# Second attention of a transformer encoder: scores two blocks ahead are issued before the transposes of the present block

## The reference

```python
for qb in range(S // Q_BLOCK):              # 8 blocks of 128 queries
    q0 = qb * Q_BLOCK
    n_keys = q0 + Q_BLOCK                   # causal by chunks of 64
    s = (jnp.einsum('bqhd,bkhd->bhqk', q_nope[:, q0:n_keys], k_nope[:, :n_keys])
         + jnp.einsum('bqhr,bkr->bhqk', q_rope[:, q0:n_keys], k_rope[:, :n_keys])).astype(F32) * scale
    p = _masked_softmax(s, _chunk_mask(q0, n_keys)[None, None])
    outs.append(jnp.einsum('bhqk,bkhe->bqhe', p.astype(v.dtype), v[:, :n_keys]))
```

## Time and profile before

| | |
|---|---|
| runs shown | 3392.67, 3393.78, 3395.44 us; median 3393.78 |
| profiled execution, its own time | 3393.93 us |
| span of its instructions | 3392.2 us (so 1.73 us lie around it) |
| TensorE busy | 2859.6 us, 84% |
| VectorE busy | 1621.3 us, 48% |
| ScalarE busy | 1252.5 us, 37% |
| GpSimd busy | 302.0 us, 9% |
| mean granted TensorE clock | 0.910 of full speed |

### The profile page before, as it was taken

How to read it: one execution, slowest core, us unless ns; L and a number is a source line. 1 busy time by engine, 2 the same in 40 slices (tenths; PEclk the granted TensorE clock), 3 DMA queues, 4 the chain that set the end, 5 groups by cost and what they waited for, 6 DMA issues and landing times. The chain is left out here.

```text
span 3392.2 us, 38273 instructions
## 1 busy us (share of the span) xinstructions
PE 2859.6 (84%) x12732; PEld 2275.8 (67%) x12732; DVE 1621.3 (48%) x2801; ACT 1252.5 (37%) x2185; POOL 302.0 (9%) x314
## 2 busy tenths in 40 slices
PE   1778888877786999999994888888785999999995
PEld 1556555654564888888873677777673788888883
DVE  3454554454335434343456377777726323232325
ACT  0355655555305212121205356656514313121213
POOL 2000000000000000000044222222100000000000
PEclk9789888887697999999996899999987999999996
DMA  5312211112311322223222111111330111111111
GB/s 199 126 41 63 63 44 60 59 56 96 123 40 37 93 74 87 85 74 95 70 67 74 22 27 27 31 29 26 114 116 13 50 50 43 49 49 49 47 40 50
DMA packets 268778, 216.65 MB, mean 64 GB/s; under 512 B 36967, under 2 KB 244118, under 8 KB 268702
## 3 DMA queue, kind: packets, MB, share of 16 engines
q1 hardware_dynamic: 251662, 156.98, 15.6%
q0 software_dynamic: 17040, 58.73, 5.6%
HBM read 186.28 MB, written 33.59 MB: 65 GB/s over the span
## 5 line engine op out<-in xcount | busy, mean ns | idle before, releaser
L1543 PE MATMUL PA<-U,W 128*128 128x512 f32 x3840 | 969.5, 409 | 143.1 <-DVE W L1031 46.2
L1543 PEld LDWEIGHTS PA<-U,W 128*128 128x128 f32 x3840 | 747.9, 197 | 317.8 <-issue 100.1
L1543 PE MATMUL SC<-U,W 128*128 128x512 f32 x2064 | 484.0, 394 | 27.4 <-DVE U L1345 23.9
L639 ACT ACTIVATE W<-raw 128x1024 fp32r<-128x1024 f32 (+1 forms) x207 | 201.2, 975 | 778.5 <-PE PA L1543 360.9
L1543 PEld LDWEIGHTS SC<-U,W 128*128 128x128 f32 x2064 | 392.8, 191 | 112.1 <-issue 26.1
L1543 PE MATMUL PA<-H,W 128*128 128x512 f32 x1536 | 355.1, 390 | 0.0
L1543 PE MATMUL SC<-H,W 128*128 128x512 f32 x1536 | 353.4, 389 | 0.0
L1543 PEld LDWEIGHTS SC<-H,W 128*128 128x128 f32 x1536 | 288.4, 188 | 59.8
L1543 PEld LDWEIGHTS PA<-H,W 128*128 128x128 f32 x1536 | 287.5, 188 | 59.6
L1031 DVE TENSOR_TENSOR W<-raw,W 128x1024 fp32r<-128x1024 f32 (+1 forms) x207 | 244.8, 1185 | 117.9 <-ACT W L639 117.3
L1113 DVE TENSOR_TENSOR H<-TB,H 128x512 fp32r<-128x512 f32 (+3 forms) x216 | 122.7, 568 | 162.3 <-ACT H L682 162.2
(11 more groups left out here) (213 smaller groups left out, 3200.5 us busy)
## 6 DMA issues: line engine op xcount, KB each, us to landing
raw<-in_ffn_w SPq DMA_DIRECT2D x128, 512.0 KB, 4.1
ada<-in_ada_w POOLq DMA_DIRECT2D x96, 512.0 KB, 4.7
U<-attention_out SPq DMA_DIRECT2D x4, 3584.0 KB, 16.8
raw<-in_da_w_qkv SPq DMA_DIRECT2D x24, 512.0 KB, 4.8
attention_out<-ostage SPq DMA_DIRECT2D x32, 256.0 KB, 2.5
X<-residual SPq DMA_DIRECT2D x2, 4096.0 KB, 16.4
attention_out<-ostage SPq DMA_DIRECT2D x64, 128.0 KB, 2.3
X<-in_x SPq DMA_DIRECT2D x2, 2048.0 KB, 9.0
```

Of the source, the lines that this page charges most:

```text
L639: nc.scalar.activation(W[:, slot, 0, 0:kt * P], raw[:, slot, 0:kt * P], ACT.Copy).then_inc(w_hi, 1)
L1543: ins = mm(bank, W[:, slot, a, kt * P:(kt + 1) * P], moving(b, kt)[:, cols], start=kt == first and (a, b) == SPLIT[0], stop=kt == last and ...
```

## The change

Two edits. In each step TensorE issues the scores of block s + 2 first and the transposes of block s second, where it was the other way round. And the probabilities get four SBUF buffers in place of two, since the exponential of block s + 2 is no longer ordered behind the transposes of block s; the two more are rows 2 and 3 of the tile X, which nothing else uses at that time. The queues of ScalarE, VectorE, GpSimd and SyncE keep their order. No instruction is added or removed.

```diff
-        prob1 = [X[:, 0, :], X[:, 1, :]]
+        prob1 = [X[:, k, :] for k in range(4)]
...
-                nc.scalar.activation(prob1[s % 2][:, 0:n], SC[s % 2][:, 0:n], ACT.Exp, bias=neg_max(s),
+                nc.scalar.activation(prob1[s % 4][:, 0:n], SC[s % 2][:, 0:n], ACT.Exp, bias=neg_max(s),
                                      accum_out=row_sum(s)).then_inc(a1["p_ready"], 1)
...
-                    ins = transpose_to(t1_bank(p, ix)[:, (b % 4) * P:(b % 4 + 1) * P], prob1[s % 2][:, b * P:(b + 1) * P])
+                    ins = transpose_to(t1_bank(p, ix)[:, (b % 4) * P:(b % 4 + 1) * P], prob1[s % 4][:, b * P:(b + 1) * P])
...
                 for s in range(NQ):
-                    turn1(h, p, s, 0)
-                    if s >= 4:
-                        turn1(h, p, s, 1)
                     if s + 2 < NQ:
                         scores1(h, p, s + 2)
                     elif proj:
                         scores1(h + 1, 1 - p, s + 2 - NQ)
+                    turn1(h, p, s, 0)
+                    if s >= 4:
+                        turn1(h, p, s, 1)
                     if s == 0:
```

## The result

The changed kernel takes 3431.01 us (median of 4 runs, 3426.14 to 3433.51) against 3394.61 us for the kernel before (4 runs): 36.4 us or 1.1% slower, ratio 1.0106 with a 95% interval of 1.0089 to 1.0124. The profiled execution took 3433.51 us, its span is 3431.8 us and its mean granted clock 0.901. The second attention holds nearly all of the difference.

What follows compares the result with a forecast made beforehand. The prediction took the chain zigzagging between ScalarE and VectorE as the bound, not TensorE. Its terms 12.2 + 1.1 + 9.9 = 23.2 us, added to 3393.9, gave 3417, 0.7% slower; the range ran from 3404 to just over 3430.

Steps and rivals of the forecast that it cites:

- step 5: Sixth step of a head: scores fill TensorE's two bank waits, TensorE arrives 0.99 us sooner, nothing waits for it; gain 0.
- step 7: Last step of a head: TensorE waits for banks and then for VectorE's L1452 as before; cost 0.
- third rival: TensorE is the bound: filled bank waits gain 0.99 us in each of 15 heads, 14.9 us, 3379; chance 0.08.
- Step 2: Third step of a head: high copy 0.87 us late behind the scores, 12.2 us over 14 heads; head 0 adds 1.1.
- steps 0 and 1: First two steps of a head: few transposes, covered by a projection of 12 matmuls before the next step; cost nothing.
- Step 4: Fifth step of a head: 0 at full clock, 1.1 us late at half clock in nine heads, 9.9 us.
- Steps 5 to 1: From the sixth step of a head into the next head's second: all costed at 0.
- more low clock: Rival: longer TensorE standstills bring low clock to all fifteen heads, 3424, or also onto steps 0 to 2, 3430; chance 0.11.

Runs made afterwards that it cites:

- scores first in all but steps 2 and 4, filled: Scores first in steps 0, 1, 3, 5, 6, 7 only, with useless matmuls ahead of the projections of steps 3 and 7: 3393.67 us, 0.9997 of the kernel before.
- Its own run: Kernel before with four probability buffers and scores issued first in step 2 alone: 3405.12 us, 1.0032.
- filled against filled: Changed kernel against kernel before, each with 12 and 6 useless matmuls ahead of the projections of steps 3 and 7: 3403.44 and 3391.51 us.
- its own run: Kernel before with four probability buffers and scores issued first in step 4 alone: 3401.82 us, 1.0020.
- maximum first: Kernel before, with VectorE taking the maximum of block s+2 first in its step, ahead of the low part of block s: 3415.60 us, 1.0070.
- both together: Changed kernel, with VectorE also taking the maximum of block s+2 first in its step: 3383.02 us, 0.9969; with useless matmuls in steps 3 and 7 added, 3368.81.

## Why the prediction was right, and where it fell short

The sign and the mechanism of the order held. I had 3417 with a range up to 3431, and the time is 3431.0, so the sum of 23.2 us was too small by 13. That the range just holds is luck in part: its upper end was the price of a rival, two of the four runs lie above it, and most of what fills it is a stretch that I had put at nothing.

**What bounds the kernel.** Right: TensorE's 87% did not make it the bound. In the run with scores first in all but steps 2 and 4, filled, the bank waits of step 5 are gone in the same way, and nothing is gained (0.9997). The 0.99 us that TensorE gains there comes back in step 7, as the wait of 0.6 us for a bank and 0.36 us more for L1452 (1.49 in place of 1.13). These bank waits stood besides only in the six heads at full clock of the kernel before, so the third rival had priced too many of them. The rule of the Trainium skill, Perfetto Trace Analysis, section Identifying the Most-Contended Engine, taken by busy time, had the sign of that rival (3379); the measurement decides, and here the rule points the wrong way, since the busiest engine was waiting for the chain.

**Step 2**, 0.87 us a head predicted. The high copy is 1.32 us behind its exponential in place of 0.67, so it is 0.65 late. The scores start 0.21 us ahead of the exponential (2340.37, 2340.58), where I had them start with the old transposes, 0.05 ahead, and they last 0.98 us and not 1.06. Its own run, with clear heads 0.7 us longer, gives 10.7 us for a sum of 13.3. A head at full clock grew by 0.8 us in all, since steps 0 and 1, which I had put at nothing, cost 0.1 to 0.2 of their own. The two errors partly cancel, which is luck, and the order as a whole, filled against filled, costs 11.9.

**Step 4.** Predicted nothing at full clock, measured nothing (31.63 us). At low clock predicted 1.1, measured 1.1 (32.95 us in its own run against 31.83 for such heads before). The number of heads was too small: I took the eight of the trace before and head 0, and it is eleven and head 0. With 1.2 us in eleven heads, less the 0.2 that low clock cost in eight before, that is an estimate of 12 us against 9.9.

**Steps 5 to 1, the term that was mis-sized.** I wrote of step 5 that TensorE "arrives 0.99 us sooner at a place where it then waits longer, in step 7", and costed that at 0. TensorE does wait longer there, 2.1 us in place of 1.2, and the new low stretch follows that standstill in eight heads. It lies over steps 0 and 1, where TensorE has no lead, and costs 0.9 to 2.3 us each, 13 in all by the distances, which is about what the sum lacks. Filling the standstill in step 7 takes the stretch away and 14.1 us off the time (3431.01 - 3416.95). That the growth of the standstill brings the stretch is borne out by all runs (none at 1.5 us or less, some at 1.7 and more), but not isolated by one of its own. I had named it in a rival, "more low clock", with four heads and 6 us on top of low clock in all fifteen; the real case is in between on step 4 and above it on steps 7 to 1. The steps 0 and 1 that I had called covered are not, least of all once the clock is at half: the high copy waits 0.71, 1.20 and 0.52 us there.

**The share of the clock.** In my sum 9.9 of 23.2 us hung on low clock. The runs give 24.5 (27.6 - 3.1) of 36.4, two thirds. The Trainium skill, TensorE: Matmul & The Clock Gate, section HAM oscillation, tells of a clock that falls in each turn of a loop because of one recurring wait. The trace agrees in part: the wait of step 3 recurs in every head and the clock falls in eleven of fourteen, and with the waits filled it stays at 1.00.

**What was to show it.** The high copy of step 2 waits for the transposes; clear heads grew by 0.8 us; the bank waits of step 5 are gone; the maximum does not wait; and the wait for L1452 grew. Heads with low clock grew by about 2 us against clear ones of before, as said, and some by 4.2. The wait for the weight split grew by 7.8 us in the window, where I had said 12; each grew by 0.8 us, but the window holds 13 of them in place of 14.

## What to carry to other kernels

Ahead of issuing work earlier on a queue, look whether anybody waits for that work, and at what it is put in front of: here the scores were never late and the transposes had 0.2 us to spare. When two engines' queues feed each other, an order on one asks for the matching order on the other; scores first lost 36 us, maximum first lost 21, and both together gained 12. Of TensorE, whose clock fell behind its waits here, cost not only the wait but also the work that follows it at half speed, and ask how much slack that work has: low clock in step 4 cost 0.2 us a head in the order of before, 1.1 to 1.4 with scores first and 1.7 with only the maximum first.

## What the hardware showed that I had not expected

Adding work made the kernel faster: 18 matmuls without use a head took 27.6 us off the changed kernel, 3.1 off the kernel before and 14.2 off the one with the maximum first. TensorE's standstills, of 2.3 to 3.2 us in step 3 and of 1.7 to 2.1 us in step 7, were followed in many heads though not all by a stretch at 1.2 GHz, of some 3 us and in some heads about twice that; those of 1.2 to 1.5 us in step 7 never were. But equal standstills did not fare alike: behind one of 3.15 us the clock fell in one head and not in the next. What tips it there was not tried by itself.
